# Router logits in four column groups, a decay product placed later, and a gather's scaling shared by two engines

## The reference

```python
q_dec = qf * jnp.exp(b)             # b: cumulative log decay, b = cumsum(log_sigmoid(a_low @ w2 + b2) / 16)
k_dec = kf * jnp.exp(-b)
...
def expert_choice_moe(h, w_router, w_gate, w_up, w_down):
    cap = EC_CAPACITY * T // N_EXPERTS                  # 64 latent rows, 32 context rows an expert
    aff = jax.nn.softmax((h @ w_router).astype(jnp.float32), axis=-1)
    top_w, top_idx = lax.top_k(aff.transpose(0, 2, 1), cap)
    xg = jax.vmap(lambda hb, ib: hb[ib])(h, top_idx)
    hid = silu(xg @ w_gate) * (xg @ w_up)
    ye = hid @ w_down * top_w
    return scatter_add(ye at top_idx)
```

## Time and profile before

| | |
|---|---|
| three runs | 2789.05, 2791.91, 2792.27 us (median 2791.91) |
| the profiled execution, its span | 2793.24 us, 2791.4 us |
| TensorE busy | 2531.3 us, 91% |
| VectorE, ScalarE busy | 1047.5 us (38%), 684.7 us (25%) |
| HBM traffic | mean 208 GB/s over the span |
| mean granted TensorE clock | 0.957 of full speed |

### The profile page before, as it was taken

One profiled execution on the slowest core, in us unless ns is written; L12 is line 12 of the kernel. 1 busy time (PEld: TensorE's weight loads), 2 busy tenths in 40 slices (PEclk: granted clock), 3 DMA queues, 4 the chain that ended last, 5 costly groups with the idle time before them and its releaser, 6 DMA issues. The chain is left out here.

```text
span 2791.4 us, 42248 instructions
## 1 busy us (share of the span) xinstructions
PE 2531.3 (91%) x17542; PEld 1624.7 (58%) x17542; DVE 1047.5 (38%) x2285; ACT 684.7 (25%) x1346; POOL 87.8 (3%) x145
## 2 busy tenths in 40 slices
PE   5999999999898499998999789989899869999997
PEld 3888877777676434443444468877677643433432
DVE  4534354344773312223222464446347431111112
ACT  3611132221532112112121252224235220100101
POOL 1000100000000000000100000010000000000000
PEclk9999999999998599999999989999999969999999
DMA  5111456255631389896988511132226159999996
GB/s 205 54 46 31 112 193 206 75 168 171 227 120 61 128 328 363 306 388 268 371 337 346 198 39 46 46 99 72 68 72 189 61 196 410 409 409 410 410 409 275
DMA packets 241826, 580.70 MB, mean 208 GB/s; under 512 B 11462, under 2 KB 120240, under 8 KB 240624
## 3 DMA queue, kind: packets, MB, share of 16 engines
q1 hardware_dynamic: 232160, 550.21, 53.0%
q0 software_dynamic: 9488, 27.90, 3.1%
HBM read 554.94 MB, written 23.13 MB: 207 GB/s over the span
## 5 line engine op out<-in xcount | busy, mean ns | idle before, releaser
L935 PE MATMUL ps<-h_hi,m_lo 128*128 128x512 f32 (+1 forms) x1152 | 346.8, 372 | 1.7 <-DVE arena L2049 1.7
L1324 PE MATMUL ps<-arena 128*32 128x512 f32 x2304 | 341.7, 601 | 6.3 <-issue 6.3
L1325 PE MATMUL ps<-arena 128*32 128x512 f32 x768 | 341.3, 601 | 0.0
L908 PE MATMUL ps<-m_lo,h_hi 128*128 128x256 f32 (+1 forms) x1248 | 237.6, 292 | 5.5 <-DVE m_lo L2022 3.9
L935 PEld LDWEIGHTS ps<-h_hi,m_lo 128*128 128x128 f32 x1152 | 208.7, 190 | 54.0 <-issue 17.0
L1324 PEld LDWEIGHTS ps<-arena 128*32 128x32 f32 x2304 | 93.8, 111 | 225.2 <-issue 223.7
L908 PEld LDWEIGHTS ps<-m_lo,h_hi 128*128 128x128 f32 x1248 | 197.2, 196 | 17.1 <-issue 12.4
L935 PE MATMUL ps<-h_lo,m_lo 128*128 128x512 f32 (+1 forms) x576 | 205.6, 357 | 0.0
L1461 PE MATMUL ps<-arena 128*64 128x512 f32 x832 | 187.3, 597 | 11.9 <-DMA arena<-in_moe_w_up 8.8
L908 PE MATMUL ps<-m_lo,h_lo 128*128 128x256 f32 (+1 forms) x624 | 177.7, 285 | 0.0
L908 PE MATMUL ps<-h_hi,m_lo 128*128 128x512 f32 (+1 forms) x512 | 143.4, 357 | 10.8 <-DVE h_lo L2125 10.6
(11 more groups left out here) (367 smaller groups left out, 4435.8 us busy)
## 6 DMA issues: line engine op xcount, KB each, us to landing
arena<-in_moe_w_down SPq DMA_DIRECT2D x120, 1024.0 KB, 9.2
arena<-in_moe_w_gate SPq DMA_DIRECT2D x116, 1024.0 KB, 10.0
arena<-in_moe_w_up SPq DMA_DIRECT2D x116, 1024.0 KB, 10.4
ring<-in_w_in SPq DMA_DIRECT2D x42, 1024.0 KB, 5.4
arena<-in_ada_w SPq DMA_DIRECT2D x40, 1024.0 KB, 5.6
mix_spill<-arena POOLq DMA_DIRECT2D x48, 256.0 KB, 2.8
x_sb<-in_moe_w_gate SPq DMA_DIRECT2D x12, 1024.0 KB, 14.1
oT<-in_moe_w_up SPq DMA_DIRECT2D x12, 1024.0 KB, 16.1
```

The costliest lines, as they stand in the source:

```text
L908: last = mm(to, stationary, moving, start=at == 0 and k == 0, stop=at == 2 and k == KD - 1)
L935: last = mm(to, w[:, k, cols], h[:, k, seg], start=n == 0 and k == 0, stop=n == 2 and k == KD - 1)
L1324: mm(ps[r][32 * b:32 * b + 32, :], c_xg[:, k, j, 32 * b:32 * b + 32], w, start=k == 0, stop=k == KD - 1)
L1325: last = mm(ps[r][96:128, :], c_xg[:, k, j, 32 * r:32 * r + 32], up[:, kk, 512:1024], start=k == 0, stop=k == KD - 1)
```

## The change

It has four parts.

1. The router is now the stationary operand (32 columns of it, of which 16 count), and `hT` is the moving one, 512 latent or 256 context columns at a time. Piece k goes to column group k % 4 of the array, so that pieces k and k + 4 add up on the same 32 partitions of `ps0` (latent) or `ps1` (context). Pieces 0 to 3 are issued between the turned pieces 5 and 6, and pieces 4 to 7 behind piece 7. The four partial sums then have to be added: VectorE copies 112 partitions of both banks to `lgT`, TensorE turns them (112 columns a token tile), and VectorE adds the four groups into `aff`, by a copy and three additions per bank.
2. The search for the largest values runs for context and latent rows together: latent experts on partitions 0 to 15, context experts on 32 to 47, in one buffer that is set to -1 beforehand. The four context rounds of their own go, and the four steps behind them run once over 512 columns. The slots are turned out of both places, and copied by two copies.
3. In the gates' stage decay product 3 moves behind job 2 of `gv`, product 2 behind the last job of `gqk`, and the keys' transposes from behind jobs 1 and 4 of `gv` to behind 3 and 5.
4. In layer 0's gathers ScalarE keeps the even pieces, and VectorE takes the odd ones, behind the first two `results_low`.

```diff
@@ behind_job
-                return [("z", u) for u, at in enumerate(((2, 3, 5, 7), (2, 3, 4, 5))[l]) if at == i]
-            return {1: [("ke", 0)], 4: [("ke", 1)], 8: [("ke", 2)], 11: [("ke", 3)]}.get(i, [])
+                return [("z", u) for u, at in enumerate(((2, 3, 7), (2, 3, 5))[l]) if at == i]
+            return {2: [("z", 3)], 3: [("ke", 0)], 5: [("ke", 1)], 8: [("ke", 2)], 11: [("ke", 3)]}.get(i, [])
@@ norm_transposes (PE)
+                def logits(ks):
+                    for k in ks:
+                        pe.wait_ge(h_lat, before("h_lat", l) + k + 1)
+                        last = mm(ps[0][32 * (k % 4):32 * (k % 4) + 32, :], routers[:, E * k:E * k + 32], hT[:, k, LAT], start=k < 4, stop=k >= 4)
+                    if CTX_NORMS[s]:
+                        for k in ks:
+                            pe.wait_ge(h_ctx, before("h_ctx", l) + k + 1)
+                            last = mm(ps[1][32 * (k % 4):32 * (k % 4) + 32, 0:CTX], routers[:, E * k:E * k + 32], hT[:, k, CX],
+                                      start=k < 4, stop=k >= 4)
+                    return last
...
+                    if k == 5:
+                        logits(range(4))
+                logits(range(4, KD)).then_inc(lg_up, 1)
@@ route (PE)
+                pe.wait_ge(lgT_ok, before("lgT_ok", l) + 1)
                 for t in q_tiles(l):
-                    for k in range(KD):
-                        last = mm(ps[0][:, t * E:(t + 1) * E], hT[:, k, tile(t)], router[:, k, :], start=k == 0, stop=k == KD - 1)
+                    bank, at = (ps[2], t - CT) if t >= CT else (ps[3], t)
+                    last = tr(bank[:, LG_ROWS * at:LG_ROWS * at + LG_ROWS], lgT[0:LG_ROWS, tile(t)], ident[0:LG_ROWS, 0:LG_ROWS])
                 last.then_inc(lg_up, 1)
@@ gather (PE)
-                        pe.wait_ge(xg_sum_ok, before("xg_sum_ok", l) + g * KD + (dt - 2))
+                        pe.wait_ge(xg_odd_ok if (dt - 3) % 2 else xg_sum_ok, g * (KD // 2) + ((dt - 3) // 2 + 1))
@@ grouped (ACT), both gathers
-                        for dt in range(KD):
+                        for dt in range(0, KD, 2):
                             gathered(g + 1, dt)
@@ grouped (DVE)
+                def gathered(g, dt):
+                    dve.wait_ge(xg_up, g * KD + (dt + 1))
+                    for s in range(2):
+                        c, n = ((0, CAPL), (CAPL, CAPC))[s]
+                        last = v.tensor_scalar(c_xg[:, dt, :, c:c + n], ps[dt % 3][:, GE * c:GE * (c + n)].rearrange("p (a b) -> p a b", a=GE),
+                                               scl[:, 1, dt, s:s + 1], modT[l][:, 24 + dt, s:s + 1], ALU.mult, ALU.add)
+                    last.then_inc(xg_odd_ok, 1)
...
                     results_low(g, YE_SPLITS[:2])
+                    if not final:
+                        for dt in range(1, KD, 2):
+                            gathered(g + 1, dt)
                     results(g, GE - 1)
@@ routing (DVE)
-                lg = ps[0][:, q0 * E:NT * E].rearrange("p (t e) -> p t e", e=E)
+                if NSEG[l] > 1:
+                    v.tensor_copy(lgT[0:LG_ROWS, CX], ps[1][0:LG_ROWS, 0:CTX])
+                v.tensor_copy(lgT[0:LG_ROWS, LAT], ps[0][0:LG_ROWS, :]).then_inc(lgT_ok, 1)
+                dve.wait_ge(lg_up, before("lg_up", l) + 2)
+                for bank, t0, n in ((ps[3], 0, CT), (ps[2], CT, NT - CT))[2 - NSEG[l]:]:
+                    groups = bank[:, 0:LG_ROWS * n].rearrange("p (t r) -> p t r", r=LG_ROWS)
+                    last = v.tensor_copy(aff[:, t0:t0 + n, :], groups[:, :, 0:E])
+                    for g in range(1, 4):
+                        link(last)
+                        last = v.tensor_tensor(aff[:, t0:t0 + n, :], aff[:, t0:t0 + n, :], groups[:, :, 32 * g:32 * g + E], ALU.add)
+                    link(last)
+                lg = aff[:, q0:NT, :]
...
-                for i, seg in enumerate(segs):
-                    for _ in range((CAPL, CAPC)[i] // 8):
-                        link(v.max(top8[0:E, i, :], work[0:E, seg]))
-                        link(v.match_replace(work[0:E, seg], top8[0:E, i, :], work[0:E, seg], -1.0))
+                for n in range(CAPL // 8):
+                    r = slice(0, both if n < CAPC // 8 else E)
+                    link(v.max(top8[r, 0, :], work[r, :]))
+                    link(v.match_replace(work[r, :], top8[r, 0, :], work[r, :], -1.0))
```

More of the change, by code:

```diff
@@ L119 @@
 K_ALL = K_ROW + NT
+LG_ROWS = 32 * 3 + E
 ADA_COLS = 4
@@ L802, in _ @@
         def _(pool):
[L803 to L804 removed]
+            nc.gpsimd.memset(mst[:, :, :], 1.0)
+            nc.gpsimd.memset(router[:, KD, :], 0.0).then_inc(p_used, PAIR_SLOTS)
             for l in range(DEPTH):
                 if l:
[L807 removed]
+                    pool.wait_ge(lg_up, before("lg_up", l))
                 rows = ((R_AB, 48, a["ada_b"][l]), (R_N1, 8, a["norm1"][l]), (R_N2, 8, a["norm2"][l]), (R_C, 8, a["c"][0]),
@@ L2301, in grouped @@
                 rows_found(0)
+                for dt in range(1, KD, 2):
+                    gathered(0, dt)
                 turn(0, True, False)
```

80 lines of the change are left out of this document (40 added, 40 removed).

## The result

The changed kernel takes 2765.48 us (median of four runs, 2763.25 to 2765.93), the kernel before 2792.09 beside it: ratio 0.9904, 95% interval 0.9887 to 0.9921. That is 26.6 us less by the medians and 27.4 us by the spans of the profiled executions (2791.4 and 2764.0 us). A gain of 30.5 us had been forecast, to 2761.4 us. The time lies in the predicted range, 4.1 us over the point. By the spans the gain missed the forecast by 3.1 us.

The account below looks back on a forecast made before the run. Experts' stages, bound by TensorE in layer 0 and transfers in layer 1, were taken to move with their start behind router and gather; 10.75 + 4.8 + 8.9 + 3.8 + 3.2 + 1.2 - 2.1 = 30.5 us, giving 2761.4 us, range 2755 to 2769.

Parts of the forecast that it names:

- The reading of the brackets: Ahead of both layers' experts: a layer's whole expert stage moves with its start, so idle brackets lie on the path.
- Router, layer 0: Layer 0, first router product to VectorE's first step: 17.75 us become 7.0, gain 10.75 us.
- the bound for a high clock: Layer 0's router: gain of 12 us if the clock stays high.
- the rival had put 12.9: Router, both layers: column groups don't overlap, 12.9 us less gain, 2774 us; chance 0.05.
- Search: Layer 0, first context round to slots' transposes: 7.83 us become layer 1's 2.87, gain 4.8 us after a second copy.
- Router, layer 1: Layer 1's router: 13.14 us become 4.25, gain 8.9 us, bounds 7.4 and 9.7.
- First gather: Layer 0's first gather, 7.6 us, with two readers: TensorE sets the pace, gain 1.2 us.
- Gates: Gates' stage: moved jobs shorten TensorE's waits; gain 3.8 us in layer 0 (3.0 to 4.7), 3.2 us in layer 1.
- The three turn boundaries: Layer 0's three later gathers: VectorE comes only after its low parts; -0.7 us each, -2.1 us for three.
- The waits come back: Rival: every boundary costs 2 us and product 3 meets a new wait of 2 or 3 us; 2768.5 us, chance 0.13.
- Slower via the clock: Rival, layer 0's experts: longer boundary waits leave TensorE at 1.2 GHz; 61 us more low clock eats the gain; chance 0.02.
- The switches between transposes and column groups: Changed norm and router: four more switches a layer, 0.14 us each, 1.1 us in all, left inside roundings.

Follow-up runs that it names:

- run 10: Changed kernel with all eight router pieces one after the other in one column group, adding up in one bank: 2774.75 us, ratio 0.9937.
- Run 6: Kernel before the change with 24 always-met waits (12 instructions) ahead of layer 0's experts on TensorE, moving its loop: 2792.71 us, ratio 1.0001.
- run 12: Kernel before the change with only the new places of the decay products and the keys' transposes: 2785.45 us, ratio 0.9975.
- run 2: Changed kernel with ScalarE scaling all pieces in all four gathers: 2765.66 us, ratio 0.9902.
- run 11: Changed kernel with the first half of the router products behind the last turned piece, ahead of the second half: 2765.64 us, ratio 0.9909.
- run 3: Changed kernel with VectorE scaling the odd gathered pieces ahead of the low parts at a turn's end: 2757.92 us, ratio 0.9878.
- run 7: Changed kernel with VectorE scaling odd pieces ahead of the low parts, plus 32 always-met waits ahead of layer 0's experts on TensorE: 2756.60 us, ratio 0.9865.
- runs 5 and 7: 32 always-met waits ahead of layer 0's experts on TensorE, in the changed kernel (5: 2765.71 us) and with odd pieces ahead of low parts (7: 2756.60 us).

## Why the prediction was right, and where it was off

**The reading of the brackets was right.** A layer's experts move with their start. Layer 1's router gave 9.0 us and its experts returned 0.6 of them, with transfers at 409 GB/s in both kernels.

**Router, layer 0.** 12.0 us against 10.75, right at the bound for a high clock. The granted clock was 0.60 in the stretch of the old router products and 1.00 from 901 to 909 in the new ones. The transposes took 0.8 us for 1.3, the rest came as counted: copies 1.1, small steps 1.9. The column groups overlap, and run 10 shows their price: 9.1 us, where the rival had put 12.9 by ideal counts.

**Search.** 5.0 against 4.8. A round does cost by its columns and not by its partitions.

**Router, layer 1**: 9.0 against 8.9, and part of this fit is luck. The 13.11 us of the earlier trace rows are of one execution, in which the clock fell 0.8 us behind the first router product. Run 6 does the same work here with the same code, and there it fell 2.7 us behind it:

```profile
2242.92 11.43 PE L1293 MATMUL ps<-router,hT 128*128 128x16 f32 x64 [0.87 <-ACT hT L1635]
```

The stage took 19.15 us there and 19.62 in run 12, in place of 21.40. Measured from those, the gain is 6.7 or 7.2 us. In layer 0 the three agree (26.77, 26.77 and 27.05).

**First gather**: 6.16 us, where the prediction's terms (5.1 and 1.1) add up to 6.2; the gain was 1.4 us, and the 1.2 that it names is a slip of 0.2.

**Gates.** Layer 1 as forecast: TensorE goes on 63.93 us into the layer, with `gv`, in place of 66.98, with product 3, so 3.05 us sooner of the 3.2. In layer 0 the low part was ready at 104.2 and not 103.6: ScalarE's high part began at 100.00, since the copy of job 6 stood at 99.05. The wait was 1.14 us, and the clock stayed high, which I had counted half. `gv` started 3.7 us sooner, where 4 to 5 had been named. The stage gave 3.2 us in the changed kernel, 5.0 when the jobs were put back and 4.3 alone. The ten profiled executions with the changed kernel's jobs and operands reach the norm at 893.4 to 896.1 us, so the gain is 2.3 to 5.0 us and 3.8 lies inside of that. Layer 1's stage takes 632.9 to 634.5 us in them, and 635.7 and 637.0 in two executions of the order of before (run 6 and the kernel before), so its 3.2 us are known to about 1.5.

**The three turn boundaries, the step that failed in size.** "-0.7 each, -2.1 us for three." They lost 1.20, 1.26 and 0.88. The cause was the named one: piece 4 turned at 5.37 us behind the gather's start where 5.42 had been worked out. What I took too low was what follows. Pieces 5 to 7 wait for nobody, but run at the low clock: piece 7 starts 1.98 us behind piece 4, where I had given 1.45, and `down` 0.78 us behind that. So `down` begins past the 7.2 to 8.0 us that I had given it at two boundaries (8.13 and 8.13), and inside at the third (7.76), where piece 4 still ran at the high clock.

**The loop's jump, which is in no term.** It cost 3.4 us. The prediction put it at nothing without a word: it does not mention the 4.68 us of TensorE ahead of turn 2, nor what a shorter program does to it. The router's 96 records of layer 0 became 32, six transposes came in, each with a weight load, and the loop's first instruction moved up by 117, from 156 instructions ahead of a block's border to 17.

**The rivals.** "The waits come back" had 2 us a boundary and a new wait ahead of product 3. The boundaries lost 1.1 us each, and ahead of product 3 there is no wait (113.18, 1658.38). "Slower via the clock" did not come: at the boundaries the low clock lasted 3.4 us as before. It lasted 6.9 us longer behind the jump, which the rival does not name, where 61 us would have eaten the gain. By run 2, the shared scaling is worth nothing net as it was written: in place of -0.9 (1.2 less 2.1) it gave -1.8 in the trace.

**The switches between transposes and column groups.** The prediction counted 0.14 us each from a row, 1.1 us in all. The Trainium skill, TensorEngine Tiling (Array Packing), Tiling Modes, Key Properties, says that a change of mode drains TensorE. By the prediction's assumption of 0.42 us each, an estimate from a row, the eight were 3.4 us. Taking two of the four new switches of a layer away with run 11 shortened the stages by 0.7 and 0.6 us, 0.3 us a switch together with what the inserted half cost. No run separates the two, and neither figure is shown. No drain of 0.42 us shows as such: the first router product starts 0.31 us behind the last transpose (900.66 and 900.97).

**Open.** Why the clock stays low for 10.3, 6.7 or 3.4 us around the jump was not taken apart further. The gaps ahead of it differ, and so does where they lie.

## What to carry to other kernels

Read a bracket for the list of the engine that it names: a piece of work given to a second engine comes when that engine's list reaches it, so put it ahead of what nobody waits for (run 3: 7 us by the ratios). Any edit that changes the length of an engine's program moves the loops behind it against the borders of its instruction blocks: look at the "issue" gaps ahead of a loop's first product in both traces before looking for causes in the data flow. And where an engine on the critical path loops only two or three times, write the loop out: here that took 10.6 us out of the turn behind the jump, and 9.6 us off the median of run 7, which stood beside it on the same chip and jumps.

## What the hardware showed that I had not expected

- A jump back in TensorE's loop stops it for 4.7 to 5.0 us while the transfers run at 400 GB/s. A target 17 instructions ahead of a block's border brings a second gap of 0.75 to 1.33 us (seven kernels), and a target one instruction ahead of it makes the one gap 3 us longer (runs 5 and 7).
- The blocks can be counted in the trace, as packets of 16 KB on queue 8. The next block lands 3 us behind the first, and six products at the low clock (1.93 us) don't cover that.
- The unrolled turn runs at a granted clock of 1.00 through 145 us, where with the jump it is 0.97.
- `MAX8` and its replacement cost the same on 48 partitions as on 16 (0.69 and 0.68 us).
